# The first unit pair behind each norm of the second block, as three split products instead of one full product

## What is computed

```
for l in range(DEPTH_2):          # DEPTH_2 = 2
    g = norm_g[l]
    f = _swiglu(_rmsnorm_2(x, g[0]), gate[l, 0], up[l, 0], down[l, 0])
    x = x + 0.5 * _rmsnorm_2(f, g[1])
    m = _mixer(_rmsnorm_2(x, g[2]), w_in[l], ..., w_out[l])
    x = x + _rmsnorm_2(m, g[3])
    f = _swiglu(_rmsnorm_2(x, g[4]), gate[l, 1], up[l, 1], down[l, 1])
    x = x + 0.5 * _rmsnorm_2(f, g[5])
```

## Time and profile before

| | us |
|---|---|
| median of 3 runs | 2516.22 |
| lowest and highest | 2514.97, 2518.14 |
| the profiled execution | 2514.94 |
| its span in the trace | 2513.1 |

### The profile page before, as it was taken

The page is one execution under the profiler, slowest core; times in us unless marked ns, Lnnn a source line. Parts: engine busy times, 40 slices in busy tenths (PEclk is TensorE's granted clock), DMA queues, the critical chain, the costliest instruction groups (busy, mean ns, idle before and its releaser), DMA issues.

```text
span 2513.1 us, 32584 instructions
## 1 busy us (share of the span) xinstructions
PE 2475.0 (98%) x11268; PEld 1980.1 (79%) x11268; DVE 1310.6 (52%) x1830; ACT 908.9 (36%) x1294; POOL 972.2 (39%) x384
## 2 busy tenths in 40 slices
PE   6999999999999999999999999999999999999998
PEld 3878778887788887778788888788887778788886
DVE  8865767256330348668531348430348668531344
ACT  3444543234321334554431333331334554431231
POOL 1332424443344443233344443344443333344443
PEclk8999999999999999999999999999999999999999
DMA  5222643322233231222233232233231322232232
GB/s 229 96 73 78 218 182 126 109 100 84 75 104 105 100 106 61 84 84 101 67 104 105 100 105 73 77 110 103 94 108 60 90 83 96 72 105 91 92 105 79
DMA packets 69702, 253.37 MB, mean 101 GB/s; under 512 B 8928, under 2 KB 11104, under 8 KB 68480
## 3 DMA queue, kind: packets, MB, share of 16 engines
q1 hardware_dynamic: 69632, 252.46, 29.8%
HBM read 244.76 MB, written 2.10 MB: 98 GB/s over the span
## 4 chain that ended last, share of the span: by engine, by line
PE 86%; issue 10%; POOL 2%; DVE 1%; DMA 0%; ACT 0%; SPq 0%; POOLq 0%; DVEq 0%; ACTq 0%
PE unit_bank L511 26%; PE unit_bank L513 26%; PE unit_bank L512 26%; PE score L597 3%; POOL w_lo L473 2%; PE mix L653 1%; PE out_bank L633 1%; PE score L902 1%; PE mix L553 0%; PE mix L661 0%; PE out_bank L558 0%; PE mix L558 0%; PE stat_bank L566 0%; PE score L653 0%; PE mix L566 0%
## 5 line engine op out<-in xcount | busy, mean ns | idle before, releaser
L473 POOL TENSOR_TENSOR w_lo<-raw,w_hi 128x1024 fp32r<-128x1024 f32 (+2 forms) x376 | 967.0, 2572 | 1519.9 <-ACT w_hi L950 1519.9
L511 PE MATMUL unit_bank<-u_hi,w_hi 128*128 128x512 f32 x2160 | 849.8, 393 | 4.0 <-POOL w_lo L473 4.0
L950 ACT ACTIVATE w_hi<-raw 128x1024 fp32r<-128x1024 f32 (+2 forms) x376 | 417.0, 1109 | 1202.2 <-PE unit_bank L513 1175.6
L513 PE MATMUL unit_bank<-u_hi,w_lo 128*128 128x512 f32 x2160 | 841.6, 390 | 0.0
L512 PE MATMUL unit_bank<-u_lo,w_hi 128*128 128x512 f32 x2160 | 841.6, 390 | 0.0
L511 PEld LDWEIGHTS unit_bank<-u_hi,w_hi 128*128 128x128 f32 x2160 | 405.7, 188 | 106.4 <-issue 16.0
L513 PEld LDWEIGHTS unit_bank<-u_hi,w_lo 128*128 128x128 f32 x2160 | 405.8, 188 | 85.1
L512 PEld LDWEIGHTS unit_bank<-u_lo,w_hi 128*128 128x128 f32 x2160 | 405.9, 188 | 84.7 <-issue 1.9
L511 PE MATMUL unit_bank<-h_hi,w_hi 128*128 128x512 f32 x992 | 387.0, 390 | 0.2 <-DVE h_lo L1765 0.2
L513 PE MATMUL unit_bank<-h_hi,w_lo 128*128 128x512 f32 x992 | 386.0, 389 | 0.0
L512 PE MATMUL unit_bank<-h_lo,w_hi 128*128 128x512 f32 x992 | 385.9, 389 | 0.0
(11 more groups left out here) (314 smaller groups left out, 1891.7 us busy)
## 6 DMA issues: line engine op xcount, KB each, us to landing
raw<-in_w_gate_up SPq DMA_DIRECT2D x168, 512.0 KB, 3.4
raw<-in_w_down SPq DMA_DIRECT2D x64, 704.0 KB, 4.1
raw<-in_w_in SPq DMA_DIRECT2D x66, 512.0 KB, 3.5
raw<-in_w_up SPq DMA_DIRECT2D x30, 512.0 KB, 3.4
f<-in_w_ada_rows SPq DMA_DIRECT2D x26, 512.0 KB, 4.9
raw<-in_w_out SPq DMA_DIRECT2D x24, 512.0 KB, 3.5
raw<-in_w_down SPq DMA_DIRECT2D x16, 512.0 KB, 3.5
ada_in_u<-in_w_ada SPq DMA_DIRECT2D x4, 1024.0 KB, 10.8
```

The lines of the kernel that those rows point to most:

```text
L473: e.tensor_tensor(w_lo[:, s, 0:n], raw[:, s, 0:n], as32(w_hi[:, s, 0:n]), ALU.subtract).then_inc(lo_ready, 1)
L511: e.matmul(bank[:], wh, hi(k), start=n == 0, stop=False)
L513: mm = e.matmul(bank[:], wl, hi(k), start=False, stop=last)
L950: e.activation(w_hi[:, s, 0:n], raw[:, s, 0:n], ACT.Copy).then_inc(hi_ready, 1)
```

## The change

The first pair behind each of the six norms with `ahead` becomes a split product. Its weights get a high part `first_hi` (ACT, placed in slots 6 to 9 of `arena`) and a low part `first_lo` (POOL, written over `first_raw`), both made among the last two pairs ahead of the norm. In the pause POOL makes `u_lo` of chunks 0 to 5 and DVE only of chunks 6 and 7. PE has 6 products per chunk in place of 2 full ones, the one with `u_lo` a chunk behind. The small steps for the new factor come earlier (DVE behind chunk 1, ACT's root behind chunk 2 and into PSUM, DVE's reciprocal behind chunk 4, PE's spread behind chunk 4); ACT's refill of side 1 moves behind the eighth chunk; PE has 6 filler products (`keep_warm`) ahead of the pair, not 3.

```
# POOL
-                    if s == 0:
-                        split_pairs(mix2(l) + 1, MIX2_PAIRS, D)
+            def split_next(r, last, n, p):
+                for s in range(2):
+                    e.wait_ge(first_hi_ready, 2 * r + s + 1)
+                    e.tensor_tensor(first_lo[:, s, :], first_raw[:, s, :], as32(first_hi[:, s, :]),
+                                    ALU.subtract).then_inc(first_lo_ready, 1)
+                split_pair(last, n)
+                split_one(p, 0, D)
+                for c in range(DC - 2):
+                    e.wait_ge(uhi_ready, DC * (2 + r) + c + 1)
+                    e.tensor_tensor(u_lo[:, c, :], u_all[:, c, :], as32(u_hi[:, c, :]),
+                                    ALU.subtract).then_inc(u_ready, 1)
+                split_one(p, 1, D)
...
# PE, norm
-                keep_warm(3)
-                for s in range(2):
-                    e.wait_ge(first_loaded[s], 16 * (FIRST_OF_NORM + r + 1))
-                for c in EIGHT:
-                    e.wait_ge(u_full, DC * r + c + 1)
+                keep_warm(6)
+                def first_low(c):
+                    e.wait_ge(u_ready, DC * (2 + r) + c + 1)
                     for s in range(2):
-                        mm = e.matmul(score[s][:], first_raw[:, s, c * P:(c + 1) * P], u_all[:, c, :],
-                                      start=c == 0, stop=c == DC - 1)
+                        mm = e.matmul(score[s][:], first_hi[:, s, c * P:(c + 1) * P], u_lo[:, c, :], start=False,
+                                      stop=c == DC - 1)
...
-                    if c == 6:
+                e.wait_ge(first_lo_ready, 2 * r + 2)
+                for c in EIGHT:
+                    e.wait_ge(uhi_ready, DC * (2 + r) + c + 1)
+                    for w in (first_hi, first_lo):
+                        for s in range(2):
+                            e.matmul(score[s][:], w[:, s, c * P:(c + 1) * P], u_hi[:, c, :],
+                                     start=c == 0 and w is first_hi, stop=False)
+                    if c:
+                        first_low(c - 1)
+                    if c == 4:
                         spread(2 * r + 2, inv_u, mix[1])
+                first_low(DC - 1)
# ACT, norm
-                with e.Fori(0, DC // 2 - 1) as i:
+                def pair(i):
                     for s in range(2):
                         refill(p + i + 1, s, D if r in (2, 5) or r == 0 else RING)
                         f_squares(p + i, s, part, 2 * i + s, g)
+                with e.Fori(0, DC // 2 - 2) as i:
+                    pair(i)
+                if ahead:
+                    for s in range(2):
+                        e.wait_ge(first_loaded[s], 16 * (FIRST_OF_NORM + r + 1))
+                        e.activation(first_hi[:, s, :], first_raw[:, s, :], ACT.Copy).then_inc(first_hi_ready, 1)
+                pair(DC // 2 - 2)
...
-                    if c == 1:
-                        refill(p + 1, 1)
-                    if c == 5:
+                    if c == 2:
                         e.wait_ge(grown_ready, r + 1)
                         token_root(root_u, x_sum)
+                refill(p + 1, 1)
# DVE, norm
-                    if c == 3 and ahead:
+                    if c == 1 and ahead:
...
-                    if c == DC - 1 and ahead:
+                    if c == 4 and ahead:
...
-                for c in range(DC):
+                e.wait_ge(u_ready, DC * (2 + r) + DC - 2)
+                for c in range(DC - 2, DC):
```

More of the change, by code:

```diff
@@ L127, in program @@
         w_lo = sb("w_lo", [P, 2, RING], F32R)
+        arena_at = nc.sbuf_base
         arena = sb("arena", [P, 26 * T])
@@ L153, in program @@
         f_sq, gf_sq, f_acc, cross, cross_acc, gf_acc = (slot(n) for n in range(6))
-        root_f, root_u, inv_f, inv_u, scaled = (slot(11)[:, 128 + 4 * n:132 + 4 * n] for n in range(5))
+        root_f, inv_f, inv_u, scaled = (slot(11)[:, 128 + 4 * n:132 + 4 * n] for n in range(4))
         x_sum = stat[:, 0:TB]
@@ L159, in program @@
         ffn_g, ffn_s, ffn_u, ffn_h = slot(6), slot(7), slot(8), slot(9)
+        first_hi = nc.alloc_sbuf_tensor_at("first_hi", [P, 2, D], F32R, offset=arena_at + 6 * T * 4)
+        first_lo = nc.alloc_sbuf_tensor_at("first_lo", [P, 2, D], F32R, offset=arena_at + 12 * T * 4)
         a_pad = arena[:, 10 * T:10 * T + T + 2]
@@ L204, in program @@
         square_sum, gf_sum, cross_sum, grown = out_bank[:, 0:TB], mix[0][:, 0:TB], mix[0][:, TB:2 * TB], mix[0][:, 2 * TB:3 * TB]
+        root_u = mix[0][:, 3 * TB:4 * TB]
         z_bank = banks[3:7]
@@ L214, in program @@
         first_loaded = [sem(f"first_loaded{i}") for i in range(2)]
+        first_hi_ready, first_lo_ready = sem("first_hi_ready"), sem("first_lo_ready")
         first_done, first_taken = sem("first_done"), sem("first_taken")
@@ L469, in _, with split_one @@
         def _(e):
+            def split_one(p, s, n):
+                e.wait_ge(hi_ready, 2 * p + s + 1)
+                e.tensor_tensor(w_lo[:, s, 0:n], raw[:, s, 0:n], as32(w_hi[:, s, 0:n]),
+                                ALU.subtract).then_inc(lo_ready, 1)
             def split_pair(p, n):
                 for s in range(2):
-                    e.wait_ge(hi_ready, 2 * p + s + 1)
-                    e.tensor_tensor(w_lo[:, s, 0:n], raw[:, s, 0:n], as32(w_hi[:, s, 0:n]),
-                                    ALU.subtract).then_inc(lo_ready, 1)
+                    split_one(p, s, n)
             def split_pairs(p0, pairs, n):
@@ L481, in _ @@
             split_pairs(MERGE1, DC // 2, 6 * P)
-            split_pairs(OUT1, LAYER0 - OUT1, D)
+            def split_next(r, last, n, p):
[10 more added lines that the diff above has]
+                split_one(p, 1, D)
+            split_pairs(OUT1, LAYER0 - OUT1 - 1, D)
             for l in range(LAYERS):
@@ L485, in _ @@
                     for half in range(2):
-                        p0, skip = ffn2(l, s, half), 1 - half
+                        p0, skip = ffn2(l, s, half), 2 - 2 * half
+                        if half == 0:
+                            split_next(3 * l + 2 * s, p0, D if s or l == 0 else RING, p0 + 1)
                         split_pairs(p0 + skip, HALF2 - skip, D)
-                        split_pairs(p0 + HALF2, DC // 2, RING)
+                        rest = half == 0 or (l == LAYERS - 1 and s == 1)
+                        split_pairs(p0 + HALF2, DC // 2 if rest else DC // 2 - 1, RING)
                     if s == 0:
-                        split_pairs(mix2(l) + 1, MIX2_PAIRS, D)
+                        split_next(3 * l + 1, mix2(l), RING, mix2(l) + 1)
+                        split_pairs(mix2(l) + 2, MIX2_PAIRS - 2, D)
             for n, c in enumerate(POOL_SUMS):
```

## The result

| | before | after |
|---|---|---|
| median (lowest to highest), us | 2515.43 (2514.35 to 2518.76), 9 runs | 2522.06 (2519.94 to 2528.67), 9 runs |
| ratio, with its 95% interval | | 1.0029 (1.0021 to 1.0038) |
| the profiled execution | 2514.94 | 2519.94 |
| its span | 2513.1 | 2518.1 |
| POOL's busy time and instructions | 972.2, 384 | 1055.6, 432 |

The changed kernel is 0.3% slower; the forecast was 2520.9 us. The profiled executions differ by 5.0 us. The medians differ by more, 6.6. TensorE's clock may be a part of that: its mean, as granted, is 0.994 in the profiled execution of before, 0.992 in that of after and 0.989 in the slowest of after (2528.67 us). But the execution that gives the median (2522.06 us) has 0.993, so the clock doesn't account for all of it.

What follows compares the result with a forecast made beforehand. PE, with work in 98% of the span, was taken as the bound. Terms: r = 0 -1.25, r = 1, 4 0, r = 3 -0.95, r = 2, 5 +6.9: +4.7 us, so 2519.6 profiled, 2520.9 median (2517.5 to 2524; with rivals 2511 to 2526).

Steps and rivals of the forecast that it cites:

- Pause of r = 1 to 5: Pause of these norms: PE waits for chunks 1 to 3, then is bound by itself; gain 0.95 us.
- Pause of r = 0: Pause of the norm out of the first block, with ACT as the feeder: gain 1.95 us.
- r = 0, last pairs: Last pairs ahead of norm 0: PE waits 0.7 us (0 to 1.5) for POOL; net gain at r = 0 1.25.
- Mixers (r = 1, 4): Mixers behind norms 1 and 4: POOL's split holds DVE's copy L1942, so gain 0 (0.95 if not held).
- r = 3: Norm 3: last pairs cost 0, the pause's gain stays: -0.95 us.
- r = 2, 5: Last pairs: PE waits 1.9 us, DVE is held, norm 4.4 late; less 0.95, loss 3.45 us each.
- Rival 1: DVE's lag is absorbed; r = 2 and 5 lose only PE's wait of 1.05 us; 2512.3 us; chance 0.18.
- rival 2: All last-pair splits are hidden and every pause pays in full: 6.7 us less, 2509.5 us; chance 0.10.
- Rival 3: At r = 2 and 5 POOL's next-pair split holds DVE's sum 2.4 us more each: 2525.7 us; chance 0.14.

Runs made afterwards that it cites:

- x_inter: Changed kernel with POOL's order before every norm altered to take turns: `first_lo` of a side, then `w_lo` of that side; 2523.76 us, ratio 1.0026.
- x_spread: Changed kernel with `first_hi` and `first_lo` made one pair earlier before norms r = 0, 2 and 5; 2528.60 us, ratio 1.0047.
- b_one: Kernel before with one extra, unused GpSimd subtraction (128x1024) before norms r = 2 and 5; 2529.07 us, ratio 1.0050.

## Why the prediction held, step by step

The sum of the steps was +4.7 us for the profiled execution; 5.0 came, 5.28 of them in the ledger and -0.28 from start-up.

- **Pause of r = 1 to 5:** forecast 0.95 each, measured 1.04. PE waits for ACT's `u_hi` (0.41 at 996.89) and is then bound by itself, as worked out.
- **Pause of r = 0:** forecast 1.95, measured 1.81.
- **r = 0, last pairs: this term was wrong.** Forecast 0.7 (0 to 1.5), measured 1.72, outside its bounds. Start-up put this program 0.27 earlier. With that allowed for, PE was free when I had it, but POOL was done 0.5 later (607.51), since its splits run at 2.8 each where DVE comes in between, and PE started 0.25 behind POOL's end. That makes the idle of 1.43. The rest is in how a stop is counted: from the start of the last product ahead of it to the start of the next it is 1.81 in place of 0.23, and the product after that follows only at 0.31. Net: -0.09, not -1.25. x_inter and x_spread, where PE doesn't wait here, have none of the 1.72. POOL's rows there:

```profile
599.00 5.67 POOL L496 TENSOR_TENSOR first_lo<-arena,first_hi 128x1024 fp32r<-128x1024 f32 x2
604.63 5.72 POOL L478 TENSOR_TENSOR w_lo<-raw,w_hi 128x1024 fp32r<-128x1024 f32 x2
```

- **Mixers (r = 1, 4):** forecast 0, because the copy L1942 would be held by POOL's split. It is: 2.29 us for two, and q's instruction at 1007.79. Given back 0.55 to 0.69 of 1.04, so -0.4 each. POOL's split ran where I had it (t = 14.4 to 16.8), but the copies ended at 17.1, not at about 17.4, and L2105 began at 17.3, not at 17.6. The page of the Trainium skill weighed there (SBUF — State Buffer, Who interferes with whom) lets such a copy contend only in a mode with two ports; this copy, at about five times the price it had with POOL idle (0.47 for two before), contends. In which mode it ran no run shows.
- **r = 3:** forecast -0.95, measured -1.0. Nothing ahead of it was late, as for r = 1 and 4.
- **r = 2, 5:** forecast 4.4 late, PE waiting 1.9; measured 4.65 and 2.07. The take of chunk 7, forecast at 1191.3, came at 1190.72, in a program that stood 0.8 earlier by then (-0.37 at N1, then the pause and the mixer): 0.2 off.
- **Rival 1 and 2** (lag absorbed, all hidden) are out by the trace itself. **Rival 3** (POOL's split of the next pair ahead of DVE's sum): at 1189.81 it took 2.87, as in the earlier trace rows, so the race did not turn. (In rival 2, what had to fit in 6.2 us ahead of U5 is three splits, not five.)

The whole came nearer than its parts. The last pairs of r = 0 and their pause were 1.2 worse than forecast, the two mixers together 0.8 better, and that these two nearly cancel is luck. Norms 2 and 5 carry the forecast: +7.2 in place of +6.9.

Two things in the forecast were right for less than the whole reason. I treated each hold as a price of its own that DVE's idle time can pay off; x_spread and b_one show that a lag moves the later splits onto other operations, so extra splits aren't additive. In after the extra splits stand so close to the norm that only one later split (at 1178.60) falls under this. And I had no clock in the sum. The median is 1.6 us further from before's than the profiled execution is (6.6 against 5.0). The clock may be a part of that, but isn't shown to be: the execution at 2522.06 us has the higher mean clock of the two (0.993 against 0.992), and there is no trace of it. A shift of start-up of up to 2 us would do as well.

## What to carry to other kernels

An engine at 42% busy is not free: before giving GpSimd another two-operand instruction, look at which VectorE instruction with two SBUF inputs will lie beside it, how soon after its start that one comes, and whether VectorE has idle time *behind* it before the next one. Where VectorE is nearly full, one 2.4 us subtraction cost 4.4 us at the norm; where it has room (r = 0), the same work was free once moved one pair earlier. Cut two traces at the same events and compare stretch by stretch: that showed losses of 12.3 us and gains of 7.0 us inside a difference of 5.0, and led to a kernel that keeps most of the gains.
